# Gate rows' Gelu written out with Square, Tanh and VectorE products; two gated banks emptied ahead of the second half of the output projection

## The reference, cut to what matters

```python
u  = gelu(u)                                  # tanh form of Gelu; 256 x 512, the "gate rows"
v  = layernorm(gelu(v), ln_g)                 # 256 x 512
mixed = einsum('hpq,bnqhd->bnphd', w_s, v) + b_s
o_sg = u * mixed                              # gated half
o_na = neighborhood_attention(q, k, v, ...)   # attention half
y  = concat([rms(o_na), rms(o_sg)]) * out_gain
x  = x + g_a * (y @ w_out)                    # output projection, 1024 x 1024
hf = modulate(x)                              # then router and 16 experts
```

## Time and profile before

| | |
|---|---|
| median of three runs | 1543.82 us |
| the profiled execution's own time | 1545.43 us |
| its span, first to last instruction | 1543.5 us |
| granted TensorE clock, mean over the span | 0.995 |
| TensorE matmul / VectorE / ScalarE / GpSimd busy | 1512.8 / 1182.5 / 956.5 / 82.0 us |

### The profile page before, as it was taken

One profiled execution on the slowest core, in us unless ns is written; L12 is line 12 of the kernel. 1 busy time (PEld: TensorE's weight loads), 2 busy tenths in 40 slices (PEclk: granted clock), 3 DMA queues, 4 the chain that ended last, 5 costly groups with the idle time before them and its releaser, 6 DMA issues.

```text
span 1543.5 us, 20181 instructions
## 1 busy us (share of the span) xinstructions
PE 1512.8 (98%) x7928; PEld 1253.8 (81%) x7928; DVE 1182.5 (77%) x1624; ACT 956.5 (62%) x1518; POOL 82.0 (5%) x78
## 2 busy tenths in 40 slices
PE   9999999999999999999999999999998899999997
PEld 9998888888888799888788888887766778888785
DVE  7568857667888584788576689877665889999997
ACT  6577854655444464878456545444367468888884
POOL 0010000000000000100000000000200000000005
PEclk9999999999999999999999999999999999999999
DMA  7535436437776455453445378884421449999994
GB/s 290 211 142 207 146 136 222 149 120 280 258 269 242 150 185 189 156 190 127 170 184 200 132 269 320 337 301 155 168 103 55 163 187 360 373 384 367 378 366 151
DMA packets 52200, 339.33 MB, mean 220 GB/s; under 512 B 7835, under 2 KB 8477, under 8 KB 13316
## 3 DMA queue, kind: packets, MB, share of 16 engines
q1 hardware_dynamic: 48932, 331.79, 57.9%
q0 software_dynamic: 3168, 6.20, 1.1%
HBM read 332.82 MB, written 10.49 MB: 222 GB/s over the span
## 4 chain that ended last, share of the span: by engine, by line
PE 48%; DVE 5%; ACT 2%; issue 1%; POOL 0%; DVEq 0%; ACTq 0%
PE bank L856 14%; PE bank L858 14%; PE bank L857 14%; PE bank L862 3%; DVE wls L2348 1%; DVE h L2318 1%; PE bank L1398 1%; PE bank L1196 0%; PE bank L1174 0%; PE bank L1113 0%; PE bank L1376 0%; PE bank L1136 0%; DVE arena L2327 0%; ACT arena L1626 0%; ACT whs L1642 0%
## 5 line engine op out<-in xcount | busy, mean ns | idle before, releaser
L2348 DVE TENSOR_TENSOR wls<-raw,whs 128x1024 fp32r<-128x1024 f32 x432 | 514.0, 1225 | 152.0 <-ACT whs L1642 151.1
L1642 ACT ACTIVATE whs<-raw 128x1024 fp32r<-128x1024 f32 x432 | 435.8, 1052 | 187.5 <-PE bank L858 165.1
L856 PE MATMUL bank<-whs,P1h 128*128 128x512 f32 (+1 forms) x732 | 290.8, 397 | 2.0 <-issue 2.0
L858 PE MATMUL bank<-whs,P1l 128*128 128x512 f32 (+1 forms) x732 | 285.2, 390 | 0.0
L857 PE MATMUL bank<-wls,P1h 128*128 128x512 f32 (+1 forms) x732 | 284.2, 388 | 0.0
L856 PE MATMUL bank<-whs,P0h 128*128 128x512 f32 (+1 forms) x620 | 247.2, 399 | 1.9 <-DVE sm L2324 1.9
L858 PE MATMUL bank<-whs,P0l 128*128 128x512 f32 (+1 forms) x620 | 241.2, 389 | 0.0
L857 PE MATMUL bank<-wls,P0h 128*128 128x512 f32 (+1 forms) x620 | 240.7, 388 | 0.0
L856 PEld LDWEIGHTS bank<-whs,P1h 128*128 128x128 f32 x732 | 138.0, 188 | 29.9 <-issue 3.3
L858 PEld LDWEIGHTS bank<-whs,P1l 128*128 128x128 f32 x732 | 137.8, 188 | 29.2
L857 PEld LDWEIGHTS bank<-wls,P1h 128*128 128x128 f32 x732 | 138.2, 189 | 26.8
(11 more groups left out here) (306 smaller groups left out, 2551.5 us busy)
## 6 DMA issues: line engine op xcount, KB each, us to landing
raw<-in_ws_dram SPq DMA_DIRECT2D x264, 1024.0 KB, 4.8
landing<-in_ws_dram SPq DMA_DIRECT2D x38, 1024.0 KB, 7.0
lnb<-in_ln_g_dram SPq DMA_DIRECT2D x6, 512.0 KB, 6.0
lnb<-in_ln_b_dram SPq DMA_DIRECT2D x6, 512.0 KB, 7.2
ydram<-arena POOLq DMA_DIRECT2D x4, 512.0 KB, 8.6
mid<-in_bias_dram SPq DMA_DIRECT2D x1, 2048.0 KB, 7.7
h<-in_x_dram SPq DMA_DIRECT2D x2, 512.0 KB, 4.0
lnb<-in_mem_dram SPq DMA_DIRECT2D x1, 1024.0 KB, 12.6
```

The costliest lines, as they stand in the source:

```text
L856: e.matmul(out, x[0], w[0], start=start, stop=False, skip_group_check=skip)
L858: return e.matmul(out, x[1], w[0], start=False, stop=stop, skip_group_check=skip)
L1642: e.activation(hi, src, ACT.Copy, bias=0.0, scale=1.0).then_inc(*high.done(n, f))
L2348: e.tensor_tensor(lo, src, f32(hi), ALU.subtract).then_inc(*low.done(n, f))
```

## The change

The Gelu of the gate rows is no longer one ScalarE instruction. ScalarE writes the square of the bank; VectorE makes (u^2 + 1/0.044715) u; ScalarE takes the tangent with a scale; VectorE makes (tanh + 1) u out of the bank, and the last product with the mixed rows has a factor 0.5. The bank of u is free after VectorE's second product, no longer after the Gelu. `sg_turn(1)`, `sg_high(1)` and `sg_low(1)` move from the first to the second tile of `so`, and with it behind step 14. On ScalarE the square sum of the gated rows of tile 0 comes before `na_high(0)`. On VectorE `gated(0, 0)` and `gated(1, 0)` move from the first tile of `mo` to the last tile of `so`, ahead of `joined`, and wait for the last scores product in place of the whole side task; `na_eps(1)` and `gated(0, 1)` move into the first tile of `mo`, ahead of `merged2(0, 0)`.

```diff
+        GELU_C, GELU_ROOT = 0.044715, float(np.sqrt(2.0 / np.pi))
...
-                ("u",), PA, x2_ready, lambda t: 2 + t, lambda t: ((act, "u", t),)))
+                ("u",), PA, x2_ready, lambda t: 2 + t, lambda t: ((vec, "ug", t),)))
...
-                at={(0, 2): lambda: sg_turn(1), (2, 4): lambda: W.feed(1), (3, 4): joined})
+                at={(1, 2): lambda: sg_turn(1), (2, 4): lambda: W.feed(1), (3, 4): joined})
...
-                put(ub[:, t, :], banks[2 + t][:, :], ACT.Gelu_apprx_tanh, "u", t)
+                put(ub[:, t, :], banks[2 + t][:, :], ACT.Square, "usq", t)
+                ac.wait_ge(vec, "ucube", t)
+                put(ub[:, t, :], ub[:, t, :], ACT.Tanh, "u", t, scale=GELU_C * GELU_ROOT)
...
-            beside = {2: [(gelu_v,)], 14: [(na_high, 0), (gate_out, 0)], 15: [(gate_out, 1)]}
+            beside = {2: [(gelu_v,)], 14: [(gate_out, 0), (na_high, 0)], 15: [(gate_out, 1)]}
...
-                (0, 2): lambda: sg_high(1), (2, 4): lambda: W.feed(1), (3, 4): joined})
+                (1, 2): lambda: sg_high(1), (2, 4): lambda: W.feed(1), (3, 4): joined})
...
             def gate_out(t):
+                ve.wait_ge(act, "usq", t)
+                stt(ub[:, t, :], ub[:, t, :], 1.0 / GELU_C, banks[2 + t][:, :], ALU.add, ALU.mult, "ucube", t)
+                ve.wait_ge(act, "u", t)
+                stt(ub[:, t, :], ub[:, t, :], 1.0, banks[2 + t][:, :], ALU.add, ALU.mult, "ug", t)
                 ve.wait_ge(vec, "ga", t)
-                ve.wait_ge(act, "u", t)
-                tt(vb[:, t, :], vb[:, t, :], ub[:, t, :], ALU.mult, "go", t)
+                ve.wait_ge(vec, "ug", t)
+                stt(vb[:, t, :], vb[:, t, :], 0.5, ub[:, t, :], ALU.mult, ALU.mult, "go", t)
...
-                wait_for(merge)
+                ve.wait_ge(mm, "sc2", 15)
...
-                (0, 2): lambda: sg_low(1), (2, 4): lambda: W.feed(1), (3, 4): joined})
+                (1, 2): lambda: sg_low(1), (2, 4): lambda: W.feed(1), (3, 2): lambda: (gated(0, 0), gated(1, 0)), (3, 4): joined})
             W.gemm_tiles("w_out_2", MIX_SEQ, OUT_AT[0], evac=merged2, at={
-                (0, 2): lambda: (gated(0, 0), gated(1, 0)), (0, 4): lambda: (W.feed(1), na_eps(1)),
-                (1, 2): lambda: (gated(0, 1), gated(1, 1)), (1, 4): lambda: W.feed(1),
+                (0, 2): lambda: (na_eps(1), gated(0, 1)), (0, 4): lambda: W.feed(1),
+                (1, 2): lambda: gated(1, 1), (1, 4): lambda: W.feed(1),
```

## The result

The changed kernel takes 1546.59 us, the median of 20 runs (1543.04 to 1551.02), beside 1543.76 us for the kernel before in 20 runs (1542.39 to 1545.45). The ratio is 1.0017, interval 1.0010 to 1.0024. That is 2.8 us slower: more than the measurement is uncertain, still within the 0.2% that I took as the bound, and 0.2 us beyond the end of my range (1546.4).

What follows compares the result with a forecast made beforehand. TensorE's matmuls fill 98% of the span, but the changed stretch was taken as bound by the chain of handovers between engines. Terms 2.13 + 1.0 - 1.2 - 2.0 = -0.1 us gave 1543.8 us, range 1541.9 to 1546.4.

Steps and rivals of the forecast that it cites:

- The serial steps at A: Gate rows of tile 0: written-out Gelu adds two products, a Tanh and three handovers, unhidden, +2.13 us; TensorE's wait becomes 3.2.
- A: Gate rows of tile 0, where TensorE waits 1.08 us before turning item 8; predicted +2.13 us serial and +1.0 clock.
- The fall at A: Gate rows of tile 0: the longer TensorE wait lowers its clock, +1.0 us, bounds nothing and 1.7.
- One sign that I had named: Exp of item 14 was to come about 14.9 us behind that of item 10, as in the kernel before.
- B: Gate rows of tile 1, two table loads on the chain: predicted -1.2 us without a clock fall, +0.25 with one.
- The serial part: Gate rows of tile 1: removed loads pay for the new steps; Exp of item 14 starts 0.1 us earlier.
- the count of loads: Gate rows of tile 1: two loads on the chain at 1.28 us each; four fewer loads in all between 1160 and 1184.
- falls at A and again at B: Rival: clock falls at both tiles' gate rows, two 1.4 us waits having only four transposes between: +1.5, 1545.3 us, chance 0.18.
- C: Projection: new VectorE order brings the scaled rows 2.0 us sooner; a clock fall there costs at most 0.4 us.
- The cover of the gated pair: Projection: `gated(0, 0)` and `gated(1, 0)` fit in VectorE's idle time before `na_low(1)`, margin 0.8 us; 2.78 us if lost.
- The new wait: Projection: TensorE waits 2.7 us before turning the scaled rows, replacing 1.90 for bank 7; its clock fall costs at most 0.4.
- The sum: Whole kernel: 2.13 + 1.0 - 1.2 - 2.0 = -0.1 us, 1543.8 us; this forecast's chance 0.33.

Runs made afterwards that it cites:

- experiment 3: Changed kernel plus 31 unused all-ones products in TensorE's waits before the turns of items 8, 12, 13 and tile 0's scaled rows: 1542.6 us, ratio 0.9995 to before.
- experiment 1: Changed kernel with the projection's old order put back, the written-out Gelu kept: 1547.56 us, ratio 1.0023 to the kernel before.
- experiment 9: Changed kernel with only tile 0's products and Tanh moved behind the reciprocal and scaling, tile 1 as changed: 1540.67 us, ratio 0.9978 to the kernel before.
- experiment 5: Changed kernel, but tile 0 of the gate rows keeps the one-instruction Gelu and its single product: 1542.64 us, ratio 0.9988 to the kernel before.
- experiment 2: Kernel before with only the projection's new order, the Gelu left as one instruction: 1541.99 us, ratio 0.9988 to the kernel before.
- experiment 4: Changed kernel with both tiles' products and Tanh moved behind VectorE's reciprocal and ScalarE's scaling: 1537.61 us, ratio 0.9961 to the kernel before.
- experiment 8: Kernel of experiment 4 with the Gelu as one ScalarE instruction and VectorE's single product per tile again: 1539.19 us, ratio 0.9965 to the kernel before.

## Why the prediction missed

**The serial steps at A: right.** Predicted +2.13 us, measured +2.08 at the scaling of item 8, and TensorE's wait is 3.19 us as forecast (3.2).

**The fall at A: right, its size too small.** From the scaling of item 8 to that of item 10 it is 7.95 us now, and it was 6.51 (1164.11 to 1170.62, by ScalarE's timeline of the kernel before). With the same steps and no fall it is 6.51 us too (experiment 3). The fall costs 1.4 us, and I had taken 1.0. It is there in all three profiles with this wait (the changed kernel twice, experiment 1). I had counted on part of it lying under the idle time. It began 0.9 us after work resumed (1167.9 against 1166.96) and cost nearly the 1.7 us of the upper bound. One sign that I had named failed by it: the Exp of item 14 is 16.25 us behind that of item 10 (1171.03 to 1187.28), not 14.9, as the fall at A lies in between.

**B: the step that failed.** The serial part was right: the Exp of item 14 comes 0.2 us earlier against the scaling of item 10, and 0.1 had been predicted. (The load that I put at 1177.86 starts at 1177.96; 0.1 us, without effect.) So was the count of loads. With a drain of 1.38 us at each load, as the Trainium skill has it ("ScalarE: Activation LUTs", section "What ACT_TABLE_LOAD costs"), it would have come another 2.8 us earlier; the measured 0.2 us decides for the 1.28 us of the rows. But the term as I used it was -1.2 us, and in it the clock no longer fell at B. It did, at waits of 1.01 and 1.41 us with four transposes between, in the two profiles of the changed kernel and in those of experiments 1 and 9. In the first three of these it fell inside the second wait: in the changed kernel's the clock is 1.00 from 1187.5 to 1188.3 and 0.50 from 1188.5, and the turn behind the wait starts at 1188.88. Measured against the kernel before, `na_low(1)` moves by +3.59 us, of which A has 3.52: B gives +0.1 in place of -1.2. The rival "falls at A and again at B" had this, with +0.25 for B, and I gave it 0.18. Had the clock stayed up, the term would have held: from the scaling of item 10 to `na_low(1)` it is 29.44 us in the kernel before and 29.51 in the changed one, both with a fall, and 28.16 in experiment 3 and 28.17 in experiment 5 (1171.03 to 1199.20), which have none. That is -1.3. I had argued from the length of one wait, and two short ones close together did the same.

**C: the order right, the price of its fall too small.** The scaled rows of tile 0 come 13.81 us behind `na_low(1)`, 1.90 us sooner than before, and -2.0 had been predicted. The cover of the gated pair held with 1.70 us to spare. The new wait of 2.80 us (predicted 2.7) brings a fall, which I had priced at 0.4 at most: the scaled rows of tile 0 are 1.69 us later than before, those of tile 1 2.39 us (1226.00 against 1223.61 by VectorE's timeline of the kernel before). It costs 0.7, and experiment 3 gives the same.

**The sum.** With the measured terms: +2.1 + 1.4 + 0.1 - 1.9 + 0.7 = +2.4 us, beside +2.8 in the medians. The forecast was -0.1. Of the 2.5 us between, 1.3 are B, 0.4 the size of the fall at A, 0.7 the fall at C, and all of them are the clock's; the serial steps were right to 0.2 us. B is more than half of it: with the clock up there, and the rest as measured, it would have been +1.1 us. As the median lies only 0.2 us beyond the range, it would have stayed inside without any one of the three.

**That it is the clock is shown by experiment 3.** It takes away the falls and none of the serial steps, and is 4.0 us faster, 3.7 of them in the four stretches where the clock had fallen. The runs themselves, each with its mean granted clock, go the same way, but prove less. Over the 32 runs of the changed kernel, one of these stretches less (3.4 us at half clock are 0.0011 of the mean) goes with about 1.1 us less time:

```
mean clock    changed kernel, us (runs)    kernel before, us (runs)
0.992         1551.0 (1)
0.993         1547.7 (12)
0.994         1546.9 (7)                   1547.2 (1)
0.995         1545.3 (6)                   1544.3 (19)
0.996         1544.6 (2)                   1544.2 (24)
0.997         1543.2 (3)                   1544.2 (15)
0.998         1545.7 (1)                   1542.5 (10)
```

The times are means. At equal clock, where both have more than one run, the two kernels differ by about 1 us at most, in both directions. They differ in how often the clock is down: 0.9943 in the mean for the changed kernel, 0.9962 for the one before (69 runs), 0.9977 for experiment 3. At 1.0 us for each 0.001 (a straight line through the 32 runs) the first two are 1.9 us apart by the clock; the same line through the 69 runs of the kernel before gives 0.5 us for each 0.001, and so 1.0 us between them. The mean takes every low stretch alike, also the last 4.4 us of the changed kernel's profile, where TensorE has no work (clock 0.50, busy 0.00), and a fall costs anything from 0.2 to 1.4 us by its place. Experiment 1 shows the limit: its mean, 0.9964, is not below that of the kernel before, and its mean time is 3.3 us above that of the kernel before on its chip.

**Where the loss sits.** From the ratios: part 2 alone is worth -1.8 us (experiment 2); adding tile 1 of part 1 leaves that where it is (experiment 5); adding tile 0 costs 4 to 4.5 us (the changed kernel). At tile 1 the loads removed pay for the steps added; at tile 0, where ScalarE waited anyway, they pay for nothing. The steps themselves cost nothing that can be measured once they stand behind the reciprocal and the scaling (experiment 4 is no slower than experiment 8, which hasn't got them). The move of `sg_turn(1)`, `sg_high(1)` and `sg_low(1)` was never run by itself.

**What stays open.** Why the clock fell at the waits of B in four profiles and not in that of experiment 5, and at the 2.80 us of C in the changed kernel and experiment 8 but not in experiments 2, 4, 5 and 9, the runs don't show. Nor do they show why the fall at the experts' start is in both profiles of the changed kernel and in before's but not in that of experiment 1, or how often each place has its fall: a profile is one execution of many.

## What to carry to other kernels

When one instruction is written out as several on two engines, look first at what is queued behind each of them: the same added steps cost 2.1 us and a fall of the clock in front of a reciprocal that TensorE waits for, and nothing behind it; the two orders (the changed kernel and experiment 4) are 9 us apart. A table load can only be worth removing where the row behind it has no wait in brackets, as at 1179.25 and 1183.93; where the next row waits anyway (0.78 us in front of 1168.94) it was free. And price a lengthened wait of the bound engine twice, once for itself and once for the clock behind it (0.7 to 1.4 us at A, B and C), also where it is cut into two shorter ones.

## What was not expected of the hardware

Two waits of 1.01 and 1.41 us with four transposes between them came with the lower clock in four of five profiles, in three of them before the second wait was over, while a single wait of 2.37 us (experiment 2) came without it, and one of 2.38 us in the kernel before with it. Work given to TensorE only to keep it busy (62 instructions in four places, 24 of them at A in 2.84 us) made the whole kernel 4.0 us faster, though it computes nothing. And a fall has no fixed price: stretches of the same length at half clock cost 1.4, 1.35, 0.7 and 0.2 us in the changed kernel.
